# New places for every stage in the order of a hybrid LRU and attention encoder block on eight cores

## What is computed

```python
h = rms_norm(x, norm1_g);  proj = h @ w_in      # 1024 -> 2560
lru_x, lru_gate, q, k, v = split(proj)          # 512 columns each
lru_x = causal_dwconv(lru_x, width 4)
lru_h = rg_lru(lru_x)                           # gates (block diagonal), exp, sqrt, linear scan over time
out_a = gelu(lru_gate) * lru_h
out_b = diff_attention(q, k, v)                 # 4 heads, two softmax maps each, block causal, T5 bias near the diagonal
x = x + concat(out_a, out_b) @ w_out            # 1024 -> 1024
h = rms_norm(x, norm2_g);  gate, val = split(h @ ffn_w_up)   # 1024 -> 2 x 3072
x = x + (gelu(causal_dwconv(gate, width 3)) * val) @ ffn_w_down
return rms_norm(x, final_norm_g)
```

## Time and profile before

| | |
|---|---|
| median of 3 runs | 1734.5 us (1732.63 to 2020.52) |
| the profiled execution's own time | 1734.59 us |
| its span, slowest core (core 3) | 1733.1 us (cores 1725.4 to 1733.1) |
| granted TensorE clock, mean of core 3 | 0.997 |
| PE busy, of it on the zero tile | 1694.0 us, 71.7 us |
| ACT, DVE, POOL busy | 1108.2, 1125.0, 282.9 us |
| moved by DMA | 342.66 MB, mean 198 GB/s |

### The profile page before, as it was taken

The page is one execution under the profiler, slowest core; times in us unless marked ns, Lnnn a source line. Parts: engine busy times, 40 slices in busy tenths (PEclk is TensorE's granted clock), DMA queues, the critical chain, the costliest instruction groups (busy, mean ns, idle before and its releaser), DMA issues.

```text
span 1733.1 us, 33350 instructions; the slowest of 8 cores (1725.4 to 1733.1 us)
## 1 busy us (share of the span) xinstructions
PE 1694.0 (98%) x10222; PEld 826.8 (48%) x10222; DVE 1125.0 (65%) x2418; ACT 1108.2 (64%) x1531; POOL 282.9 (16%) x471
## 2 busy tenths in 40 slices
PE   9989999999999999999999999999999999999998
PEld 4444444444544555455554445445554455544443
DVE  3689766545876857657557586638775377664943
ACT  6797775537875775568674687537964478832721
POOL 2143221001321101201012111111111011111000
PEclk9999999999999999999999999999999999999999
DMA  9991799955487554965348866794548653447642
GB/s 297 266 293 62 249 289 312 296 145 202 145 214 251 170 168 138 254 209 172 128 156 245 238 177 177 206 250 157 170 156 231 183 174 125 156 168 212 225 171 74
DMA packets 170271, 342.66 MB, mean 198 GB/s; under 512 B 77808, under 2 KB 77936, under 8 KB 169968
## 3 DMA queue, kind: packets, MB, share of 16 engines
q1 hardware_dynamic: 170096, 340.52, 63.9%
HBM read 268.12 MB, written 56.62 MB: 187 GB/s over the span
## 4 chain that ended last, share of the span: by engine, by line
PE 83%; DMA 6%; ACT 3%; issue 3%; DVE 2%; POOL 1%; SPq 1%; DVEq 0%; ACTq 0%; POOLq 0%
PE pb L895 46%; PE pb L913 23%; PE pb L1177 7%; PE pb L1141 4%; DMA slot<-wslab 3%; PE pb L1403 1%; DMA slot<-x 1%; PE pb L748 1%; DMA KT<-w_up 1%; ACT PT L1168 1%; DMA Va<-w_in 1%; DMA KT<-w_out 1%; ACT slot L810 0%; ACT thr L1073 0%; SPq L681 0%
## 5 line engine op out<-in xcount | busy, mean ns | idle before, releaser
L895 PE MATMUL pb<-hT,slot 128*128 128x512 bf16 x3584 | 819.3, 380 | 7.3 <-ACT raw L1015 2.2
L895 PEld LDWEIGHTS pb<-hT,slot 128*128 128x128 bf16 x3584 | 339.2, 98 | 413.0 <-issue 37.3
L1168 ACT ACTIVATE PT<-pb,prm 128x1024 bf16<-128x1024 f32 (+1 forms) x288 | 299.4, 1063 | 99.5 <-PE pb L1141 57.9
L913 PE MATMUL pb<-slot,aT 128*128 128x512 bf16 x1536 | 347.1, 379 | 3.1 <-DMA slot<-wslab 1.6
L913 PEld LDWEIGHTS pb<-slot,aT 128*128 128x128 bf16 x1536 | 147.3, 98 | 182.1 <-issue 12.5
L1310 DVE TENSOR_TENSOR aT<-pb,aT 128x512 bf16<-128x512 f32 x192 | 130.9, 687 | 105.4 <-PE pb L895 101.6
L1320 DVE TENSOR_TENSOR slot<-pb,slot 128x512 f32<-128x512 f32 x180 | 122.5, 686 | 106.4 <-PE pb L913 104.2
L1032 DVE SCALAR_TENSOR_TENSOR facc<-raw,prm,facc 128x512 f32<-128x512 f32 x192 | 143.1, 747 | 31.5 <-ACT facc L1026 22.1
L1177 PEld LDWEIGHTS pb<-Va,PT 128*128 128x128 bf16 x2176 | 137.7, 98 | 53.3 <-issue 16.0
L1015 ACT ACTIVATE raw<-pb 128x512 f32<-128x512 f32 x167 | 99.5, 596 | 97.4 <-PE pb L895 80.9
L1177 PE MATMUL pb<-Va,PT 128*128 128x129 bf16 x2176 | 157.0, 220 | 3.7 <-DVE acp L1206 1.8
(11 more groups left out here) (139 smaller groups left out, 1591.9 us busy)
## 6 DMA issues: line engine op xcount, KB each, us to landing
slot<-wslab SPq DMA_DIRECT2D x326, 512.0 KB, 5.1
slot<-x SPq DMA_DIRECT2D x80, 512.0 KB, 8.3
wslab<-slot SPq DMA_DIRECT2D x50, 512.0 KB, 8.4
out<-slot SPq DMA_DIRECT2D x28, 512.0 KB, 6.2
x<-slot SPq DMA_DIRECT2D x24, 512.0 KB, 3.5
Va<-w_up SPq DMA_DIRECT2D x20, 512.0 KB, 7.3
KT<-w_up SPq DMA_DIRECT2D x20, 512.0 KB, 7.3
KT<-w_in SPq DMA_DIRECT2D x10, 512.0 KB, 10.5
```

The costliest lines, as they stand in the source:

```text
L895: last = e.matmul(bank(p), lhsT=w[:, kk, cc * 128:(cc + 1) * 128], rhs=src[:, hf * 4 + kk, :], start=(hf == 0 and kk == 0), stop=(hf == 1 ...
L913: last = e.matmul(bank(p), lhsT=src[:, k0 + hf * 4 + kk, t * 128:(t + 1) * 128], rhs=w[:, kk, :], start=(hf == 0 and kk == 0), stop=(hf == ...
L1168: op("act", act_us(2 * N, ptr=1), lambda e: e.activation(out=PT[:, pt.s, :, 0:N], in_=psum[:, s.s:s.s + 2, 0:N], func=AF.Exp, bias=pv("far ...
```

## The change

Only the numbers of `PLAN` change; no operation is added or removed by the source, except that the zero-tile matmuls follow from the schedule.

```diff
 PLAN = {
-    "FR": {"N": (-0.854, -0.362), "A": (-0.26, 0.154), "F1": (0.136, 0.275), "G": (0.222, 0.304),
-           "F2": (0.363, 0.605), "F3": (0.748, 0.936), "L": (0.427, 0.816), "B": (-0.062, 0.576),
-           "C": (0.559, 0.733)},
-    "PR": {"N0": (-7.642, -7.896), "N1": (-6.299, -6.187), "V": (-6.658, -6.616, 0.491), "G": (-6.413, -6.498, 0.644),
-           "L0": (-6.122, -5.754), "Q": (-5.988, -5.966, 0.207), "K": (-6.015, -5.702, 0.777), "L1": (-4.943, -4.012),
-           "B0": (-6.001, -5.143), "B1": (-4.114, -2.917), "C": (-4.558, -2.74)},
-    "P": [(-4.484, -3.485), (-3.436, -2.533), (0.747, 0.854), (-0.01, 0.395), (0.921, 2.235)],
-    "E": [0.037, -0.045, -0.055, 0.047, 0.131, 0.157],
-    "WB": 0.712,
-    "S": [-7.95, -6.709, -6.709, -6.3, -5.846],
+    "FR": {"N": (-0.984, -1.059), "A": (-1.36, -1.03), "F1": (0.289, -0.239), "G": (0.249, -1.068),
+           "F2": (0.394, 0.776), "F3": (0.837, 1.271), "L": (0.485, 0.851), "B": (-0.319, -0.099),
+           "C": (1.015, 1.073)},
+    "PR": {"N0": (-10.376, -9.652), "N1": (-6.695, -5.773), "V": (-7.782, -7.869, 2.573), "G": (-8.157, -8.379, -4.388),
+           "L0": (-8.541, -5.157), "Q": (-6.616, -3.996, 1.108), "K": (-5.967, -4.761, 1.574), "L1": (-4.993, -0.33),
+           "B0": (-7.331, -6.298), "B1": (-4.037, -1.145), "C": (-15.398, -9.241)},
+    "P": [(-0.958, 3.727), (4.086, -3.898), (1.751, 4.993), (-5.264, -6.092), (0.776, 3.037)],
+    "E": [-0.123, 0.013, 0.069, 0.01, 0.279, 0.582],
+    "WB": 2.525,
+    "S": [-13.56, -7.147, -7.777, -7.81, -5.188],
 }
```

## The result

The changed kernel takes 1714.55 us (median of 4 runs, 1714.2 to 1715.24) against 1734.86 before: a ratio of 0.9888, 95% interval 0.9868 to 0.9907. That is 1.1% less; the forecast was 1717. The span of the slowest core goes from 1733.1 to 1713.0, 20.1 us less, where the sum said 17.6.

A forecast was written before the change was run, and what follows sets the result against it. The prediction took the LRU and attention chains, not PE or DMA, to bound the first part. Its terms -11.8 - 4.9 - 3.5 + 2.6 = -17.6 gave a 1715.5 us span, with 1.5 around it 1717 us; range 1690 to 1748 (forecast's own 1703 to 1729).

The forecast's parts named there:

- the sum: Whole kernel: -11.8 - 4.9 - 3.5 + 2.6 = -17.6 us, taking the span from 1733.1 to 1715.5.
- The chain behind it: Before 169 us: the LRU and attention chains, both running over ACT, bound the first part, not PE or DMA.
- the marks that the prediction set: Expected after: first L1066 near 43 us, C of group 0 near 125, the third's first gates near 150.
- the 11.8 us of the earlier weights: First part: loading L's weights one batch earlier starts the LRU chain earlier; 11.8 us gained, bounds 0 and 11.8.
- both chains that end at 169: Group 0's attention up to C and group 1's LRU, ending at the MLP's first gates; both to profit by 11.8 us.
- C ahead of all: Between C of group 0 and the first gates: no other work in between, 24.0 for 28.9 us, gain 4.9.
- K's earlier weights: First part: two write-backs and 1 MB of parameters less ahead of K's weights; 3.5 us gained, bounds 0 and 7.
- held start: Rival, chance 0.17: group 1's later LRU chunks hold the third's start, the 11.8 us are gone, about 1733 us.
- the cover: Start: V's 7.4 us of matmuls done later in place of zero-tile matmuls, so delaying x tiles costs nothing; otherwise +7.4.
- Two more table loads: First part, ACT: gelus of group 1 falling between Exps of the first LRU add two loads, 2.6 us charged.
- Groups 2 to 7: After 250 us: B ahead of the MLP, C behind it, A early; taken as 0, bounds -10 and +10 us.
- The slower rival: Chance 0.10: in every later group MLP evacuations wait behind attention's Exps and PE starves, 11 us a group, 1783 us.

The follow-up runs named there:

- V's weights: Changed kernel with V's weights and x tiles 2 and 3 again ahead of the weights of G and of L of group 0: 1745.1 us, ratio 1.0025.
- F and G: Changed kernel with the MLP and gate places F1, F2, F3 and G of groups 2 to 7 as before: 1746.8 us, ratio 1.0022.
- fifth pair of P: Changed kernel with the place of the MLP's last third of groups 0 and 1 as before (0.921 to 2.235): 1751.8 us, ratio 1.0056.
- The first part alone: Changed kernel with FR and E, the places of groups 2 to 7, as before: 1735.2 us, ratio 0.9991.
- the places of groups 2 to 7 alone: Kernel before with only FR and E as changed, its first part old: 1754.9 us, ratio 1.0100.
- run 4: Not a run's label but a verb and a size: kernels with the new first part take 4 to 16 us more than the scheduler's own estimate.

## Why the prediction was right, and where it was not

The time, its sign and the range were right: 1717 forecast, 1714.55 measured. Its working was right in part.

**What bounds the kernel: right.** Lost time of PE is the quantity that moved, and 80 to 250 us was where most of it lay: 51.5 to 35.2 us, forecast "about 34".

**The chain behind it: wrong in its sizes.** Of the marks that the prediction set, the first LRU chunk (39.4, forecast near 43) was about met. C of group 0 was forecast near 125 and came at 135.6, the gates near 150 and came at 162.2. The step that failed is that the 11.8 us of the earlier weights pass on one for one "for both chains that end at 169". The LRU kept 10 to 15 us of it for five chunks and then lost it: group 1's last projection came at 159.2 for 150.5. Attention started 1.3 us earlier and was 3.9 us shorter, and that is what C of group 0 gained. C ahead of all was sized at 4.9; from its first matmul to the gates passed 26.6 for 28.9 us, 2.3, and with its place undone the gates came no later. K's earlier weights were sized at 3.5 and did come 4.1 us earlier, though not as counted: six write-backs are issued ahead of the last of them where five were, while 1 MB of parameters and one 0.5 MB store of V (L999) moved behind. Of that, attention got 1.3 us. The loss fell all the same, for it was not only moved to an earlier start. By the timelines, the later LRU chunks and attention of group 1 now run beside the first third, with matmuls to cover them; that this is what lowers the loss is read from the rows, not tested apart. That is what the rival "held start" missed. Its condition was met (the last projection at 159.2, not before 150, from just the later places it named), and its conclusion, no gain, was not.

**The head: the cover was counted, the cost was not.** Zero-tile and idle time in the first 40 us grew by 5.0, near the bound of 7.4. It was taken at nothing because V's work is done later; it is, but the 5 us are part of what the first part gives back.

**Two more table loads: right.** ACT loads at 34.4, 44.5, 56.8 and 61.2 us, four where there were two. Timeline of ACT after:

```profile
42.93 1.53 ACT L810 ACTIVATE slot<-Va,prm 128x512 bf16<-128x512 f32 x2
44.48 1.28 ACT L1073 ACT_TABLE_LOAD   x1
45.77 0.69 ACT L1073 ACTIVATE thr<-pb,sm 128x512 f32<-128x512 f32 x1
```

From the end of the casts at 44.46 to the next Exp at 45.77 pass 1.31 us. The ScalarE: Activation LUTs page of the Trainium skill ("What ACT_TABLE_LOAD costs") gives 2.66 with its drain; in this trace the drain is not to be seen.

**Groups 2 to 7: wrong.** Taken at 0 with bounds of 10 either way; the loss behind 250 us fell by 13.7, and the prediction had itself named a change of over 10 as what would make it wrong. Two errors, some 7 us too much in the first part and 14 too little behind, met in a sum that is 2.5 us off. That part of the agreement is luck. The slower rival (attention ahead of the MLP starves PE) was wrong as to this kernel: 3.2 us are lost from 700 to 1300, less than before. With the old MLP places it is right in part: 24.4 us are lost there, and 6.0 of the 13.9 us of idle time end at an Exp.

**The form of the sum: wrong.** Costs were added step by step, as if each place acted alone. Undoing one step at a time in the changed kernel costs 7 (L of group 1), 11 (C), 21 (write-backs), 24 (V's weights), 23 (F and G) and 29 us (fifth pair of P): 115 us for six steps out of a gain of 19. The first part alone takes 2 us off, the places of groups 2 to 7 alone add 17. At the hand-over from 350 to 700 us the runs show why: a chain needs real work ready beside it, and each place decides both what is ready here and what is missing later.

What stays open: why kernels with the new first part run 4 to 16 us longer than planned where those with the old one run -2 to 6. A lower granted clock is one part by the rows: 0.96 for 0.98 in 80 to 169 us, and over the four runs of the changed kernel the nine cores at 0.998 or more took 1701.2 to 1710.6 us, the nine at 0.995 or less 1710.3 to 1713.7. That it is the cause was not tested by itself, and the kernel without the zero tile, whose clock was lower still at about the same time, speaks against its being the whole.

## What to carry to other kernels

Take the time that a "busy" engine spends on filler out of its busy time first; then a change of order alone has a ceiling (110.7 us here), and its result can be read as a change of that sum. Do not price a new set of priorities step by step: halves of a good plan can be worthless or worse, so look where one stretch hands over to the next and ask what real work is left to lie beside its chain. And an earlier start of a chain is worth only what the work that it meets on the way allows: K's weights came 4.1 us earlier and attention 1.3, and five LRU chunks led by 10 to 15 us while the last came 22 us later.

## What the runs showed of the hardware that was not expected

Without the zero-tile matmuls the granted clock of core 3 fell to 0.55 and 0.59 between 110 and 130 us, behind and beside gaps of PE, and was at 1.00 again from 140 to 180 us; yet the median of the kernel can't be told from the one with them, since the slower matmuls filled time that was idle.

In the same run two of the eight cores (4 and 5) stood at 0.81 from 40 to 80 us although PE had no gap there: 32 matmuls in a row took 8.57 us on core 4, where they take 7.07 on core 3 of the changed kernel (below, in this order). Over the whole span these two had 0.975 and 0.976 as their mean, and core 4 was the slowest core, 1727.6 us against 1705.3 on core 3.

```profile
46.06 8.57 PE L909 MATMUL pb<-slot,hT 128*128 128x512 bf16 x32
...
42.12 7.07 PE L913 MATMUL pb<-slot,hT 128*128 128x512 bf16 x32
```
